# Shift and scale columns paired in one block of a modulation weight, depth steps released two at a time, latent rows ahead of context rows

## The chip, the cores and the metric

The kernel runs on one core of a Trainium2 chip. The metric is the device time of one execution in microseconds (us), and its median over several runs. Engines: PE (TensorE, the matrix engine), DVE (VectorE), ACT (ScalarE), POOL (GpSimd) and SP (SyncE, which here only issues DMAs).

## The reference, cut to what matters

One layer of a transformer over 512 latent tokens (`SEQ`) and 256 context tokens (`CTX`) of width 2048. It begins with a modulated RMS norm, and this is the only part that the change touches:

```python
mod_lat = (silu(c) @ w_mod + b_mod).reshape(B, N_MOD, 1, D)            # latent: shift, scale, gate, shift, scale, gate
mod_ctx = (silu(c_ctx)[None] @ w_mod + b_mod).reshape(1, N_MOD, 1, D)
h  = rms_norm(x, g_norm1) * (1 + mod_lat[:, 1]) + mod_lat[:, 0]
hc = rms_norm(ctx, g_norm1) * (1 + mod_ctx[:, 1]) + mod_ctx[:, 0]
p_lat, p_ctx = h @ w_in, hc @ w_in     # columns: 512 of the latent-attention query, 320 of its key/value, then neighbourhood attention
# ... two attentions, output projection, gated residual, then an expert-choice mixture of 16 experts
```

`w_mod` is a 2048 x 12288 matrix of float32. Its first 2048 columns give the shift, the next 2048 the scale. A feature (one of the 2048 depth indices of `h`) can be modulated only when both its shift and its scale are known.

## The kernel before, in words

**Stages.** The start (to 28 us of the trace) loads the tokens transposed (`xT`, 16 depth steps of 128 partitions by 768 tokens) and sums their squares. The stage of the change follows, to 138.5 us: the shift and scale columns of the modulation, the modulated tokens, and the query projection of the latent attention. Then come the key/value and neighbourhood projections (to about 520 us), the attentions, the output projection, and from about 1141 us the experts, which end the kernel.

**The modulation.** SP loads `w_mod` in blocks of 512 columns, each in four pieces of 512 depth rows (1024 KB each, L560) into a ring of six (`MOD_RING`). A semaphore `ma_used`, counted up by PE for each piece that it has used, frees a place. `mod_quarter(pos, kq)` (L683 to L691) multiplies one piece: four matmuls of 32 x 512 outputs in four column groups of the array, which the trace counts as 8 records. After four quarters DVE copies the bank to SBUF (`take_mod`, L1549), PE turns it into columns (`mod_columns`, L702: four small matmuls with 2 moving columns, in the trace 8 records, into `MJ`), and DVE adds the bias (`mod_columns` of DVE, L1554) into `modcol`. The blocks come in the order `MOD_ORDER = [0, 4, 1, 5, 2, 6, 3, 7]`: blocks 0 to 3 are shift, 4 to 7 scale. So two positions, one shift block and one scale block, are needed before any feature is ready, and they release four depth steps at once.

**The modulated tokens.** After every second position `apply_mod(kq)` runs on DVE for the four depth steps of a group. For a depth step k it scales the 512 latent columns and the 256 context columns (L1589, semaphore `h_part`); ACT adds the shift and rounds to the fp32r format (`h_hi`, L1181, `hi_set`); DVE then makes the remainder `h_lo` (L1595, `lo_set`). The order on DVE is four scalings (two depth steps, both halves), two remainders, two scalings, and so on.

**The query projection.** `qa_step(k)` (L712 to L727) is one depth step for the four latent tiles: for each tile three matmuls of 128 x 512 (`three_passes`, L709 to L711: high x high, high x low, low x high), 12 in all, into the banks of tiles 0 to 3. It reads latent rows alone, but waits for `lo_set` of both halves of step k, and for `w_low`, the remainder of its weight block, which DVE makes (`low`, L1573) from the block that ACT has rounded (`high`, L1171). A weight block holds four depth steps.

**What sets the order.** Each engine runs its program in the written order; semaphores hold it. PE's list for this stage is written by hand around L747 to L766: positions 0 and 1 first, then for each further pair of positions the four steps of the previous group between the quarters, and the last four steps at the end. After it, a loop over `SLOTS` runs the other projections, with w_mod's later blocks done by DVE (L1642, L1647) at slots given by a table.

## Time and profile before

| | us |
|---|---|
| median of 3 runs (lowest, highest) | 2102.36 (2102.05, 2112.09) |
| the profiled execution's own time | 2099.53 |
| its span, first to last instruction | 2097.7 |
| PE busy in the span | 1952.0 (93%) |
| DVE busy | 836.2 (40%) |
| ACT busy | 427.3 (20%) |
| POOL busy | 171.5 (8%) |

PE's granted clock is 0.986 of full speed over the span. DMA moved 597.55 MB at a mean of 285 GB/s, and 427 to 428 GB/s in nearly every fortieth of the span from 1200 us on. A busy share is no limit by itself: the stage of the change is 5% of the span, and what a change there is worth is read from PE's own gaps in it and from what follows.

### The profile page before, as it was taken

The page shows a single profiled execution, that of the slowest core. Times are in us where ns is not written, and L with a number is a line of the kernel's source. Part 1 is how long each engine was busy: PE and PEld are TensorE (multiplying, and loading weights), DVE is VectorE, ACT ScalarE, POOL GpSimd, SP SyncE. Part 2 cuts the span into 40 slices and gives each one's busy share as a digit, 9 for nine tenths or more (in the row PEclk, how much of TensorE's full clock was granted, in tenths as well). Part 3 has the DMA queues.
Part 4 walks back from the last instruction along what each step waited for, and adds up shares of the span by engine and source line. Part 5 has one row for each costly group of instructions (what it writes and reads, how often), then busy time and mean ns, then how long its engine had stood idle before and what let it go on. Part 6 is the DMA issues. An engine that isn't in the chain of part 4 may idle for free.

```text
span 2097.7 us, 25991 instructions
## 1 busy us (share of the span) xinstructions
PE 1952.0 (93%) x10218; PEld 1241.5 (59%) x10218; DVE 836.2 (40%) x1721; ACT 427.3 (20%) x1141; POOL 171.5 (8%) x401
## 2 busy tenths in 40 slices
PE   4899999999999999989996999999989999998987
PEld 1578788878877777768885453534434353534432
DVE  5457887773255555534444022121303121121303
ACT  4232223222145555532222000000000000000000
POOL 0003112011133222200000000000000000000000
PEclk9999999999999999999997999999999999999998
DMA  9937888783122111222227899999999999999998
GB/s 403 404 145 274 318 301 291 273 283 141 36 103 83 44 44 44 71 105 86 100 100 297 356 391 406 428 428 427 427 428 428 427 428 428 427 428 428 427 428 311
DMA packets 75208, 597.55 MB, mean 285 GB/s; under 512 B 7360, under 2 KB 25024, under 8 KB 32336
## 3 DMA queue, kind: packets, MB, share of 16 engines
q1 hardware_dynamic: 62496, 586.92, 69.4%
q10 hardware_dynamic: 12592, 8.98, 1.3%
q8 instruction: 82, 1.34, 0.3%
q14 instruction: 38, 0.31, 0.0%
HBM read 583.27 MB, written 12.60 MB: 284 GB/s over the span
## 4 chain that ended last, share of the span: by engine, by line
PE 44%; DMA 10%; DVE 2%; issue 1%; ACT 0%; POOL 0%; POOLq 0%; ACTq 0%; DVEq 0%
PE SM L1089 8%; DMA arena<-in_w_gate_up 8%; PE TM L1089 8%; PE TM L1117 5%; PE SM L1117 5%; PE TR L1047 3%; PE MJ L1047 3%; DMA arena<-in_w_down 1%; PE SN L1076 1%; PE SM L951 1%; PE SM L953 1%; PE SM L952 1%; PE TM L951 1%; PE TM L953 1%; PE TM L952 1%; DMA wor<-in_w_out 1%
## 5 line engine op out<-in xcount | busy, mean ns | idle before, releaser
L1089 PE MATMUL SM<-arena 128*64 128x512 f32 x1024 | 244.8, 598 | 35.7 <-DMA arena<-in_w_gate_up 35.2
L1089 PE MATMUL TM<-arena 128*64 128x512 f32 x1024 | 242.5, 592 | 0.0
L1647 DVE SCALAR_TENSOR_TENSOR arena<-arena,csil 128x512 f32<-128x512 f32 x240 | 180.4, 752 | 43.8 <-DMA arena<-in_w_mod 35.5
L1089 PEld LDWEIGHTS SM<-arena 128*64 128x64 f32 x1024 | 70.5, 136 | 177.0 <-issue 175.9
L1089 PEld LDWEIGHTS TM<-arena 128*64 128x64 f32 x1024 | 76.7, 137 | 143.1 <-issue 138.4
L1117 PE MATMUL TM<-arena 128*64 128x512 f32 x512 | 116.9, 598 | 1.4 <-DMA arena<-in_w_down 1.2
L1117 PE MATMUL SM<-arena 128*64 128x512 f32 x512 | 114.6, 601 | 0.9 <-DVE arena L1959 0.9
L1383 ACT CAST y_hi<-arena 128x512 fp32r<-128x512 f32 x32 | 19.8, 619 | 385.7 <-DVE arena L1920 385.1
L1171 ACT ACTIVATE wh<-wr 128x2048 fp32r<-128x2048 f32 (+1 forms) x32 | 58.7, 1835 | 192.4 <-PE TN L711 148.8
L709 PE MATMUL SM<-wh,h_hi 128*128 128x512 f32 (+1 forms) x224 | 89.5, 400 | 7.9 <-DVE h_lo L1595 7.9
L1389 ACT CAST memberT<-MJ 128x512 fp32r<-128x512 f32 x8 | 4.7, 586 | 428.3 <-PE MJ L1062 428.3
L709 PE MATMUL TM<-wh,h_hi 128*128 128x512 f32 (+1 forms) x224 | 87.5, 391 | 0.0
L1941 DVE TENSOR_TENSOR arena<-arena,SN 128x512 f32<-128x512 f32 x56 | 38.5, 687 | 122.1 <-PE SN L1077 122.1
L710 PE MATMUL SM<-wl,h_hi 128*128 128x512 f32 (+1 forms) x224 | 86.0, 384 | 0.0
L711 PE MATMUL SM<-wh,h_lo 128*128 128x512 f32 (+1 forms) x224 | 85.9, 383 | 0.0
L711 PE MATMUL TM<-wh,h_lo 128*128 128x512 f32 (+1 forms) x224 | 85.3, 381 | 0.0
L710 PE MATMUL TM<-wl,h_hi 128*128 128x512 f32 (+1 forms) x224 | 85.2, 380 | 0.0
L1409 POOL TENSOR_TENSOR st<-st,halves 128x1 f32<-128x1 f32 (+2 forms) x116 | 81.8, 705 | 41.7 <-DVE st L1562 32.1
L1573 DVE TENSOR_TENSOR wl<-wr,wh 128x2048 fp32r<-128x2048 f32 (+1 forms) x32 | 70.0, 2188 | 33.6 <-ACT wh L1171 33.5
L1895 DVE TENSOR_TENSOR arena<-cst,rope_t 128x512 f32<-128x512 f32 x8 | 5.5, 692 | 178.9 <-PE MJ L1062 178.8
L1117 PEld LDWEIGHTS SM<-arena 128*64 128x64 f32 x512 | 35.6, 138 | 68.7 <-issue 65.2
L1117 PEld LDWEIGHTS TM<-arena 128*64 128x64 f32 x512 | 33.9, 136 | 66.7 <-issue 63.2
(318 smaller groups left out, 3509.6 us busy)
## 6 DMA issues: line engine op xcount, KB each, us to landing
arena<-in_w_gate_up SPq DMA_DIRECT2D x128, 2048.0 KB, 17.4
arena<-in_w_down SPq DMA_DIRECT2D x64, 2048.0 KB, 25.5
arena<-in_w_mod SPq DMA_DIRECT2D x96, 1024.0 KB, 5.0
wr<-in_w_na SPq DMA_DIRECT2D x24, 1024.0 KB, 6.9
wor<-in_w_out SPq DMA_DIRECT2D x8, 2048.0 KB, 7.8
xT<-in_tokens_t SPq DMA_DIRECT2D x4, 1536.0 KB, 12.8
arena<-in_w_qkv SPq DMA_DIRECT2D x8, 640.0 KB, 5.1
wr<-in_w_qa SPq DMA_DIRECT2D x4, 1024.0 KB, 12.1
```

Of the source, the lines that this page charges most:

```text
L709: pe.matmul(dst, h_hi[:, k, rows], w_hi[w % 2][:, cols], start=first, stop=False)
L710: pe.matmul(dst, h_hi[:, k, rows], w_lo[w % 3][:, cols], start=False, stop=False)
L711: return pe.matmul(dst, h_lo[:, k, rows], w_hi[w % 2][:, cols], start=False, stop=last)
L951: pe.matmul(bank(n), mix_hi[:, k, cols], wo_hi[p % 2][:, i, :], start=(i == 0), stop=False)
L952: pe.matmul(bank(n), mix_hi[:, k, cols], wo_lo[p % 2][:, i, :], start=False, stop=False)
L1047: mm = pe.matmul(dst[:, i * P:(i + 1) * P], x1[:, tile, k * P:(k + 1) * P], member[:, tile, :], start=(tile == 0), stop=(tile == LT - 1))
L1089: mm = pe.matmul(GU[b][64 * e:64 * e + CAP, :], xsT[:, k, 64 * e:64 * e + CAP], w[:, 2 * (b // 2) + e, (b % 2) * NB:(b % 2 + 1) * NB], sta ...
L1117: mm = pe.matmul(GU[2 * (i // 4) + b][64 * e:64 * e + CAP, :], actT[:, f, 64 * e:64 * e + CAP], w[:, 2 * j + e, b * NB:(b + 1) * NB], star ...
L1171: sc.activation(w_hi[w % 2][:, 0:n], w_raw[w % 3][:, 0:n], ACT.Copy).then_inc(w_high, 1)
L1409: po.tensor_tensor(out_ap, ms, halves[:, 0:n], ALU.pow).then_inc(done, 1)
L1573: ve.tensor_tensor(w_lo[w % 3][:, 0:n], w_raw[w % 3][:, 0:n], w_hi[w % 2][:, 0:n].bitcast(F32), ALU.subtract).then_inc(w_low, 1)
L1647: ve.scalar_tensor_tensor(acc, row, c, acc, ALU.mult, ALU.add).then_inc(mod_step, 1)
```

## The change

The columns of `w_mod` for shift and scale are laid out anew on the host: each block of 512 columns now holds 256 shift columns and the 256 scale columns of the same features. So every position gives both for two depth steps (`MOD_K = 2`), and `MOD_ORDER` is gone. DVE computes `mul1` for two steps at every position and applies them at once. Within a position it goes latent scaling of both steps, latent remainder, context scaling, latent remainder, context scaling, then (at even positions) the weight remainder `low`, then both context remainders. `qa_step(k)` waits for the latent remainders alone; the context ones are waited for once, at the first context tile of the key/value projection (slot 4). PE runs two `qa_step` between the quarters of every position from 1 on; at the last position one of them comes after `mod_columns`. SP issues the weight block for pos//2 ahead of the pieces of positions 2, 4 and 6 instead of behind them.

```diff
--- before.py
+++ after.py
@@ -56,7 +56,7 @@
 assert ROWS == NA_KH and P % ROWS == 0
 
 MOD_RING = 6
-MOD_ORDER = [0, 4, 1, 5, 2, 6, 3, 7]
+MOD_K = KD // (2 * MODB)
 
 HALO = NA_KW // 2 * ROWS
 WIN = P + 2 * HALO
@@ -552,14 +552,16 @@
 
             for kq in range(4):
                 sp.dma_start(xT[:, 4 * kq:4 * kq + 4, :], t["tokens_t"][kq].rearrange("p (k n) -> p k n", n=TOK)).then_inc(tok_in[kq], 16)
-            for pos, b in enumerate(MOD_ORDER):
+            for pos in range(2 * MODB):
+                if pos and pos % 2 == 0:
+                    load_w(pos // 2)
                 for kq in range(4):
                     n = 4 * pos + kq
                     if n >= MOD_RING:
                         sp.wait_ge(ma_used, n - MOD_RING + 1)
-                    sp.dma_start(mod_a[n % MOD_RING], mod_piece(b, kq)).then_inc(ma_in[n % MOD_RING], 16)
-                if pos % 2 == 0:
-                    load_w(pos // 2)
+                    sp.dma_start(mod_a[n % MOD_RING], mod_piece(pos, kq)).then_inc(ma_in[n % MOD_RING], 16)
+                if pos == 0:
+                    load_w(0)
             load_w(4)
             sp.wait_ge(ma_used, 8 * MODB)
 
@@ -717,7 +719,7 @@
                     pe.wait_ge(rb_copied, 1)
                 if j == 0:
                     pe.wait_ge(w_low, kq + 1)
-                pe.wait_ge(lo_set, 2 * k + 2)
+                pe.wait_ge(lo_set, 4 * (k // MOD_K) + k % MOD_K + 1)
                 for tile in range(LT):
                     mm = three_passes(bank(tile), k, tile, kq, j, Q_RANK, k == 0, k == KD - 1)
                     if k == KD - 1:
@@ -744,26 +746,21 @@
                 dst = RSTD_BANK[:, tile * P:(tile + 1) * P] if tile < LT else TR[:, (tile - LT) * P:(tile - LT + 1) * P]
                 pe.matmul(dst, ones[:], diag[tile % 2], start=True, stop=True).then_inc(rb_full, 1)
             mod_columns(0)
-            for kq in range(4):
-                mod_quarter(1, kq)
-            mod_columns(1)
-            for pos in range(2, 2 * MODB, 2):
-                k = 2 * pos - 4
+            for pos in range(1, 2 * MODB):
+                k = MOD_K * (pos - 1)
                 mod_quarter(pos, 0)
                 mod_quarter(pos, 1)
                 qa_step(k)
                 mod_quarter(pos, 2)
-                qa_step(k + 1)
                 mod_quarter(pos, 3)
-                qa_step(k + 2)
-                mod_quarter(pos + 1, 0)
-                qa_step(k + 3)
-                mod_columns(pos)
-                for kq in range(1, 4):
-                    mod_quarter(pos + 1, kq)
-                mod_columns(pos + 1)
-            for k in range(KD - 4, KD):
-                qa_step(k)
+                if pos + 1 < 2 * MODB:
+                    qa_step(k + 1)
+                    mod_columns(pos)
+                else:
+                    mod_columns(pos)
+                    qa_step(k + 1)
+            qa_step(KD - 2)
+            qa_step(KD - 1)
 
 
             def turn(n):
@@ -834,6 +831,8 @@
                     n = first_acc(w) + tile
                     if tile == 0:
                         pe.wait_ge(w_low, w + 1)
+                    if s == LT:
+                        pe.wait_ge(lo_set, 2 * KD)
                     if w % 4 == 0 and n >= 6:
                         before = n - 6
                         if before < V_ACC:
@@ -1175,12 +1174,14 @@
             sc.copy(rstd_b[:, SEQ:TOK], TR[:, 0:CTX]).then_inc(rb_copied, 1)
             high(0)
 
-            for k in range(KD):
+            for pos in range(2 * MODB):
                 for c, (lo, hi) in enumerate(((0, SEQ), (SEQ, TOK))):
-                    sc.wait_ge(h_part, 2 * k + c + 1)
-                    sc.activation(h_hi[:, k, lo:hi], xT[:, k, lo:hi], ACT.Identity, bias=modcol[:, k, c:c + 1]).then_inc(hi_set, 1)
-                if k % 4 == 3:
-                    high(k // 4 + 1)
+                    for i in range(MOD_K):
+                        k = MOD_K * pos + i
+                        sc.wait_ge(h_part, 4 * pos + 2 * c + i + 1)
+                        sc.activation(h_hi[:, k, lo:hi], xT[:, k, lo:hi], ACT.Identity, bias=modcol[:, k, c:c + 1]).then_inc(hi_set, 1)
+                if pos % 2:
+                    high(pos // 2 + 1)
 
 
             def squares(n):
@@ -1549,10 +1550,12 @@
                 ve.tensor_copy(moda_sum, MODBANK[pos % 2]).then_inc(ma_sum, 1)
 
             def mod_columns(pos):
-                b = MOD_ORDER[pos]
+                two = slice(MOD_K * pos, MOD_K * pos + MOD_K)
                 ve.wait_ge(ma_col, pos + 1)
-                ve.tensor_tensor(modcol[:, 4 * b:4 * b + 4, :], MJ[:, 0:8].rearrange("p (a b) -> p a b", b=2),
-                                 bcol[:, 4 * b:4 * b + 4].unsqueeze(2).broadcast_to([P, 4, 2]), ALU.add).then_inc(ma_free, 1)
+                ve.tensor_tensor(modcol.rearrange("p (s k) c -> p s k c", s=2)[:, :, two, :],
+                                 MJ[:, 0:8].rearrange("p (s k c) -> p s k c", s=2, k=MOD_K),
+                                 bcol.rearrange("p (s k) -> p s k", s=2)[:, :, two].unsqueeze(3).broadcast_to([P, 2, MOD_K, 2]),
+                                 ALU.add).then_inc(ma_free, 1)
 
             ve.wait_ge(ss_step, 1)
             ve.tensor_copy(rowsum[0:1, 0:SEQ], RSTD_BANK[0:1, :])
@@ -1574,34 +1577,38 @@
 
             HALVES = ((0, SEQ), (SEQ, TOK))
 
-            def apply_mod(kq):
-                four = slice(4 * kq, 4 * kq + 4)
-                scale = slice(KD + 4 * kq, KD + 4 * kq + 4)
-                ve.wait_ge(ma_free, 2 * kq + 2)
-                ve.scalar_tensor_tensor(mul1[:, four, :], modcol[:, scale, :], 1.0, g1[:, four].unsqueeze(2).broadcast_to([P, 4, 2]),
-                                        ALU.add, ALU.mult).then_inc(mul_set, 1)
-                ve.wait_ge(mul_set, kq + 1)
-                if kq == 0:
-                    ve.wait_ge(rb_copied, 1)
-                for k in range(4 * kq, 4 * kq + 5):
-                    if k < 4 * kq + 4:
-                        for c, (lo, hi) in enumerate(HALVES):
-                            ve.scalar_tensor_tensor(xT[:, k, lo:hi], xT[:, k, lo:hi], mul1[:, k, c:c + 1], rstd_b[:, lo:hi],
-                                                    ALU.mult, ALU.mult).then_inc(h_part, 1)
-                    j = k - 1
-                    if j >= 4 * kq:
-                        for c, (lo, hi) in enumerate(HALVES):
-                            ve.wait_ge(hi_set, 2 * j + c + 1)
-                            ve.scalar_tensor_tensor(h_lo[:, j, lo:hi], xT[:, j, lo:hi], modcol[:, j, c:c + 1], h_hi[:, j, lo:hi].bitcast(F32),
-                                                    ALU.add, ALU.subtract).then_inc(lo_set, 1)
+            def scale_part(pos, c, i):
+                k, (lo, hi) = MOD_K * pos + i, HALVES[c]
+                ve.scalar_tensor_tensor(xT[:, k, lo:hi], xT[:, k, lo:hi], mul1[:, k, c:c + 1], rstd_b[:, lo:hi],
+                                        ALU.mult, ALU.mult).then_inc(h_part, 1)
+
+            def low_part(pos, c, i):
+                k, (lo, hi) = MOD_K * pos + i, HALVES[c]
+                ve.wait_ge(hi_set, 4 * pos + 2 * c + i + 1)
+                ve.scalar_tensor_tensor(h_lo[:, k, lo:hi], xT[:, k, lo:hi], modcol[:, k, c:c + 1], h_hi[:, k, lo:hi].bitcast(F32),
+                                        ALU.add, ALU.subtract).then_inc(lo_set, 1)
 
             for pos in range(2 * MODB):
+                two = slice(MOD_K * pos, MOD_K * pos + MOD_K)
+                scale = slice(KD + MOD_K * pos, KD + MOD_K * pos + MOD_K)
                 take_mod(pos)
                 mod_columns(pos)
-                if pos % 2:
-                    apply_mod(pos // 2)
-                else:
+                ve.wait_ge(ma_free, pos + 1)
+                ve.scalar_tensor_tensor(mul1[:, two, :], modcol[:, scale, :], 1.0, g1[:, two].unsqueeze(2).broadcast_to([P, MOD_K, 2]),
+                                        ALU.add, ALU.mult).then_inc(mul_set, 1)
+                ve.wait_ge(mul_set, pos + 1)
+                if pos == 0:
+                    ve.wait_ge(rb_copied, 1)
+                scale_part(pos, 0, 0)
+                scale_part(pos, 0, 1)
+                low_part(pos, 0, 0)
+                scale_part(pos, 1, 0)
+                low_part(pos, 0, 1)
+                scale_part(pos, 1, 1)
+                if pos % 2 == 0:
                     low(pos // 2)
+                low_part(pos, 1, 0)
+                low_part(pos, 1, 1)
             low(4)
             ve.tensor_scalar(gq_b[:], gq_b[:], MLA_SCALE, None, ALU.mult).then_inc(gains_set, 1)
             ve.tensor_scalar(gqn[:], gqn[:], NA_SCALE, None, ALU.mult).then_inc(gains_set, 1)
@@ -2047,6 +2054,8 @@
         "bcol": columns(g["b_mod"][:2 * D]), "bcol2": columns(g["b_mod"][3 * D:5 * D]),
     }
     w_in = g["w_in"]
+    paired = np.arange(2 * D).reshape(2, 2 * MODB, NB // 2).swapaxes(0, 1).reshape(-1)
+    w_mod = g["w_mod"][:, np.concatenate([paired, np.arange(2 * D, 6 * D)])]
     qb = to_rows(g["w_qb"].reshape(Q_RANK, HEADS, QK).swapaxes(0, 1), HEADS)
     kvb = to_rows(g["w_kvb"].reshape(KV_RANK, HEADS, NOPE + VD).swapaxes(0, 1), HEADS)
     gate, up = (g[k].reshape(PAIRS, 2, KD, P, F_EXP) for k in ("w_gate", "w_up"))
@@ -2056,7 +2065,7 @@
         "tokens_t": to_rows(tokens.T, 4),
         "c_col": np.concatenate([columns(np.asarray(inputs["c"])[0]), columns(inputs["c_ctx"])], axis=1),
         "consts": np.concatenate([consts[n].astype(np.float32) for n, _ in CONST_SIZES], axis=1),
-        "w_mod": to_rows(g["w_mod"].reshape(D, 6 * MODB, NB).swapaxes(0, 1), 6 * MODB, 4),
+        "w_mod": to_rows(w_mod.reshape(D, 6 * MODB, NB).swapaxes(0, 1), 6 * MODB, 4),
         "b_mod": np.asarray(inputs["b_mod"]),
         "w_qa": to_rows(w_in[:, :Q_RANK], 4),
         "w_kv": to_rows(w_in[:, Q_RANK:IN_MLA], 4),
```

On PE, at the first positions before: two groups of `mod_columns` (`L702`), with position 1's 16 quarter matmuls between them, then two quarters of position 2 (`TM` is its bank, `csil` the activations) and the first query step, whose first three matmuls are shown.

```order
L702 MATMUL MJ<-cst,arena 128x2 x4
L690 MATMUL TN<-arena,csil 32x512 x16
L702 MATMUL MJ<-cst,arena 128x2 x4
L690 MATMUL TM<-arena,csil 32x512 x8
L709 MATMUL SM<-wh_62,h_hi 128x512
L710 MATMUL SM<-wl_59,h_hi 128x512
L711 MATMUL SM<-wh_62,h_lo 128x512
```

The same place now, with the lines of the changed kernel (`L704` is `L702` of before, `L692` is `L690`, `L711` to `L713` are `L709` to `L711`):

```order
L704 MATMUL MJ<-cst,arena 128x2 x4
L692 MATMUL TN<-arena,csil 32x512 x8
L711 MATMUL SM<-wh_62,h_hi 128x512
L712 MATMUL SM<-wl_59,h_hi 128x512
L713 MATMUL SM<-wh_62,h_lo 128x512
```

The first query step has moved ahead past the other two quarters of position 1, its columns, and two quarters of position 2: it now stands after two quarters of position 1.

On DVE, the first group before, from the second columns to the first remainders (`xT` the tokens, `mul` the scale, `wl_59` a weight remainder, `h_lo` the tokens' remainder):

```order
L1573 TENSOR_TENSOR wl_59<-wr_56,wh_62 128x2048
L1549 COPY arena<-TN 128x512
L1554 TENSOR_TENSOR modcol<-MJ,cst 128x8
L1581 SCALAR_TENSOR_TENSOR mul<-modcol,cst 128x8
L1589 SCALAR_TENSOR_TENSOR xT<-xT,mul,rstd_b 128x512
L1589 SCALAR_TENSOR_TENSOR xT<-xT,mul,rstd_b 128x256
L1589 SCALAR_TENSOR_TENSOR xT<-xT,mul,rstd_b 128x512
L1589 SCALAR_TENSOR_TENSOR xT<-xT,mul,rstd_b 128x256
L1595 SCALAR_TENSOR_TENSOR h_lo<-xT,modcol,h_hi 128x512
```

The same place now, a whole even position (512 wide is latent, 256 context):

```order
L1555 TENSOR_TENSOR modcol<-MJ,cst 128x2x4
L1597 SCALAR_TENSOR_TENSOR mul<-modcol,cst 128x4
L1582 SCALAR_TENSOR_TENSOR xT<-xT,mul,rstd_b 128x512 x2
L1588 SCALAR_TENSOR_TENSOR h_lo<-xT,modcol,h_hi 128x512
L1582 SCALAR_TENSOR_TENSOR xT<-xT,mul,rstd_b 128x256
L1588 SCALAR_TENSOR_TENSOR h_lo<-xT,modcol,h_hi 128x512
L1582 SCALAR_TENSOR_TENSOR xT<-xT,mul,rstd_b 128x256
L1576 TENSOR_TENSOR wl_59<-wr_56,wh_62 128x2048
L1588 SCALAR_TENSOR_TENSOR h_lo<-xT,modcol,h_hi 128x256 x2
```

Two operations less stand ahead of the first latent remainder, and the weight remainder `wl_59` has moved from the front of position 0 to behind six token operations of it.

## Rows read from the trace of the kernel before

**Rows 1.** Windows of stages: us, busy by engine, PE clock, DMA share, GB/s.

```profile
71.00:97.00 26.00, 23.19 (x135) 13.60 (x138) 12.73 (x23) 6.23 (x9) 0.00 (x0) 0.93 0.97 397
97.00:121.00 24.00, 21.10 (x128) 12.12 (x120) 12.60 (x23) 6.23 (x9) 0.00 (x0) 1.00 0.67 260
121.00:138.50 17.50, 13.73 (x48) 11.15 (x49) 10.51 (x22) 7.31 (x14) 0.79 (x3) 0.80 0.36 150
138.50:440.00 301.50, 299.00 (x1485) 250.28 (x1484) 231.55 (x295) 86.38 (x257) 59.98 (x80) 1.00 0.79 280
...
60.00:72.00 12.00, 11.18 (x77) 6.58 (x79) 3.70 (x6) 0.00 (x0) 0.00 (x0) 1.00 1.01 421
...
112.00:116.00 4.00, 4.00 (x27) 2.97 (x19) 0.00 (x0) 0.00 (x0) 0.00 (x0) 1.00 0.06 19
```

**Rows 2.** Waits of PE between 26 and 140 us: total, times, longest.

```profile
PE SM L709 <- DVE h_lo L1595: 7.9, 3, 3.9
PE MJ L702 <- DVE arena L1549: 3.3, 4, 0.8
PE TM L690 <- DMA arena<-in_w_mod: 1.5, 1, 1.5
```

**Rows 3.** Waits of PE between 140 and 440 us, the longest.

```profile
PE TR L781 <- ACT arena L1235: 2.2, 4, 0.6
```

**Rows 4.** Timeline of PE, columns of position 0, quarters of position 1: start, duration.

```profile
38.28 1.05 PE L702 MATMUL MJ<-cst,arena 128*128 128x2 f32 x8
39.27 3.92 PE L690 MATMUL TN<-arena,csil 128*32 128x512 f32 x32
```

**Rows 5.** Timeline of PE around columns of position 5 and step 8.

```profile
95.82 1.05 PE L702 MATMUL MJ<-cst,arena 128*128 128x2 f32 x8 [0.81 <-DVE arena L1549]
96.80 1.92 PE L690 MATMUL TM<-arena,csil 128*32 128x512 f32 x16
100.73 0.47 PE L709 MATMUL SM<-wh,h_hi 128*128 128x512 f32 x1 [2.00 <-DVE h_lo L1595]
...
103.64 1.06 PE L690 MATMUL TM<-arena,csil 128*32 128x512 f32 x8
```

**Rows 6.** Timeline of PE: a step, a quarter, the next step.

```profile
80.60 0.50 PE L709 MATMUL SM<-wh,h_hi 128*128 128x512 f32 x1
...
83.54 1.06 PE L690 MATMUL TM<-arena,csil 128*32 128x512 f32 x8
84.54 0.50 PE L709 MATMUL SM<-wh,h_hi 128*128 128x512 f32 x1
```

**Rows 7.** Timeline of PE: last columns, starts of steps 12 and 13, key/value projection.

```profile
119.87 1.05 PE L702 MATMUL MJ<-cst,arena 128*128 128x2 f32 x8 [0.81 <-DVE arena L1549]
124.77 0.77 PE L709 MATMUL SM<-wh,h_hi 128*128 128x512 f32 x1 [3.85 <-DVE h_lo L1595]
...
130.03 0.63 PE L709 MATMUL SM<-wh,h_hi 128*128 128x512 f32 x1
...
138.53 0.30 PE L709 MATMUL TM<-wh,h_hi 128*128 128x320 f32 x1
```

**Rows 8.** Timeline of DVE: first weight remainder, and step 8's scalings and remainders.

```profile
40.91 2.29 DVE L1573 TENSOR_TENSOR wl<-wr,wh 128x2048 fp32r<-128x2048 f32 x1 [1.37 <-ACT wh L1171]
...
97.31 2.21 DVE L1589 SCALAR_TENSOR_TENSOR xT<-xT,mul,rstd_b 128x512 f32<-128x512 f32 x4
99.44 1.14 DVE L1595 SCALAR_TENSOR_TENSOR h_lo<-xT,modcol,h_hi 128x512 fp32r<-128x512 f32 x2
```

**Rows 9.** One line's instructions on DVE: ns min/median/max, first and last start.

```profile
L1595 DVE SCALAR_TENSOR_TENSOR h_lo<-xT,modcol,h_hi x32: 477/616/755, 47.6 to 129.4; 128x512 fp32r<-128x512 f32 x16, 128x256 fp32r<-128x256 f32 x16
```

**Rows 10.** Timeline of ACT: first weight block, and step 8's and 9's sums.

```profile
38.95 1.92 ACT L1171 ACTIVATE wh<-wr 128x2048 fp32r<-128x2048 f32 x1
...
98.10 2.18 ACT L1181 ACTIVATE h_hi<-xT,modcol 128x512 fp32r<-128x512 f32 x4 [17.41 <-DVE xT L1589]
```

**Rows 11.** Timeline of SP's queue: key/value weight blocks.

```profile
120.33 31.01 SPq L551 DMA_DIRECT2D wr<-in_w_kv  x3
```

## The prediction

> **What bounds the kernel now.** I read the windows by stage first, then PE's waits, then the timelines of PE, DVE and ACT in the stage of the change. From 71 to 121 us PE is busy nearly throughout while DMA falls from a share of 0.97 to 0.67, and from 112 to 116 us DMA moves almost nothing though PE still has the last quarters to do [rows 1]. So the end of this stage is set by PE and by what PE waits for, not by the weights' transfer. From 138.5 to 440 us PE is busy 299.0 of 301.5 us, with DMA at 0.79 [rows 1] and a longest group of waits of 2.2 us in all [rows 3]: whatever time the stage of the change gives to PE reaches the stages behind it, which run in PE's order. The reader should therefore ask one question: when does PE begin the key/value projection, at 138.53 us before [rows 7]?
>
> PE's waits in the stage are 7.9 us for the token remainder `h_lo` (three waits: 2.0, 2.0 and 3.85), 3.3 us for the copy of a modulation bank (four of 0.81) and 1.5 us for one piece of `w_mod` [rows 2, 5, 7], 12.7 us in all. Its clock is a second cost: the mean granted clock is 0.93 from 71 to 97 us and 0.80 from 121 to 138.5 us, against 1.00 between [rows 1]. At the tail PE idles 3.85 us, and step 12 then takes 130.03 - 124.77 = 5.26 us [rows 7], at the level of 1.2 GHz; step 8, at 2.4 GHz, takes 103.64 - 100.73 = 2.91 us [rows 5].
>
> **What the change costs and moves.** The sum of the work stays. PE has the same 32 quarters, 8 columns groups and 16 steps. DVE has the same 64 token operations and four more small `mul1` (it runs 8 instead of 4, of half the width, beside PE's quarters); ACT has the same. So the sum is PE's order walked through with the durations before.
>
> The building blocks, on PE: columns to the next quarter 96.80 - 95.82 = 0.98 us; two quarters behind columns 1.92 us [rows 5]; a step behind a quarter 83.54 - 80.60 = 2.94 us, and a quarter behind a step 84.54 - 83.54 = 1.00 us, so a pair behind a step about 1.93 us [rows 6]; a step behind a step (138.53 - 130.03) / 3 = 2.83 us [rows 7]. On DVE: the first scaling starts 97.31 - 95.82 = 1.49 us after PE's columns start [rows 5, 8]. Two token operations, one latent and one context, are issued in (99.44 - 97.31) / 2 = 1.065 us [rows 8]; they last 0.755 and 0.477 us [rows 9], so they overlap by 0.085 each, and the latent one takes 0.67 us of DVE, the context one 0.39.
>
> *One position (2 to 6).* Counted from the start of the columns before it: scalings from 1.49 us, both latent ones issued by 2.83. ACT starts its first sum 98.10 - 97.31 = 0.79 us after the first scaling, and of 2.18 us for two latent and two context sums [rows 8, 10] a latent one has some 0.67 us, so it ends at 2.95; the remainder can start at about 3.05, ends at 3.80, and PE starts 0.15 later, as before (99.44 + 1.14 to 100.73 [rows 5, 8]): 3.95. PE's own work is done at 0.98 + 1.92 = 2.90, so it waits 1.05 us. Before, the wait was 2.00 us per pair of positions, so halving the chain saves nothing over two positions; the copy's 0.81 us, however, was open once per pair and is now under a step of 2.9 us. A position is then 3.95 + 2.91 (step) + 1.93 (quarters) + 2.94 (step) = 11.73 us.
>
> *The first position.* Here the change adds a wait. The weight remainder of block 0 ran on DVE at 40.91 us [rows 8], before anything else needed DVE; now it is queued behind six token operations. DVE scales from 38.28 + 1.49 = 39.77 us [rows 4], ACT is on the weight block until 38.95 + 1.92 = 40.87 [rows 10] and then makes the first sum by 41.54, and from 41.6 DVE issues two remainders and two context scalings, 2 x 0.67 + 2 x 0.39 = 2.1 us, then the weight remainder of 2.29 us [rows 8]: 46.0, and step 0 at 46.2. PE has done its two quarters at 39.27 + 1.93 = 41.2 [rows 4] and waits 5.0 us. Behind step 0 in PE's order are quarters 6 and 7 and with them two places of the ring.
> After a longer gap than the tail's 3.85 us I take step 0 at the tail's 5.26 us [rows 7]; at full clock it would be 2.91. So: 46.2 + 5.26 + 1.93 + 2.94 = 56.3 us for the start of position 1's columns.
>
> *To the end.* Five positions: 56.3 + 5 x 11.73 = 114.9, columns of position 6. The last position: 3.95 + 2.91 + 1.93 = 8.79, and 0.81 for the copy, which no step covers here: columns at 124.5. Step 13 lies in the wait for the last remainders (0.98 + 2.94 = 3.92 against 3.95), which before stood open for 3.85 us, and steps 14 and 15 follow: 124.5 + 3.95 + 2 x 2.83 = 134.1 us. Against 138.5 that is 4.4 us gained. By kind: waits 5.0 + 6 x 1.05 + 0.81 = 12.1 us against 12.7, so almost nothing; the rest is clock, where two of the stretches at 1.2 GHz fall away (the one between 71 and 97 us and the tail's) and one comes at step 0. Bounds: step 0 at full clock gives 6.7 us; each further step at 1.2 GHz costs 5.26 - 2.91 = 2.35 us.
>
> **What hides the other edits.** *DMA:* a load of 1024 KB at 421 GB/s [rows 1] takes 2.5 us; nine per pair of positions are 22.5 us against 2 x 11.73 = 23.5 on PE. PE stays the slower. While it waits for step 0 the ring holds pieces up to the eleventh, and the queue runs on. Even if transfers set the pace, the last piece would land near 112 us as before [rows 1], ten before it is needed. Moving three weight blocks ahead of four pieces delays these by 2.5 us, inside that lead. *DVE at the end:* from 126.0 the eight token operations take 4 x 0.67 + 4 x 0.39 + 0.2 = 4.4 us, then the remainder of the first key/value block, about 1.5 us: 132, two before PE needs it at 134.1; the wait for context rows stands four tiles later and is free. *SP:* the loads of the next key/value blocks, issued at 120.33 us [rows 11], depend on the last quarter and move to about 125; two pieces and the block need 2 x 2.5 + 1.6 us, so it lands by 134, while PE wants its remainder a whole block of six tiles after 134. If these covers failed, each costs its own lateness, under 3 us.
>
> The profiled execution took 2099.5 us and lies 2.9 under the median; its sum is 2099.5 - 4.4 = 2095.1, and at the median 2102.4 - 4.4 = 2098.0 us.
>
> **Rivals.** *Full cover:* if DVE's chain is met by PE's quarters at positions 2 to 7, 6 x 1.05 = 6.3 us more go, 10.7 in all: 2091.7. For it speaks only that 1.05 us is a small difference of four durations; against it, that the same chain left 2.0 us before [rows 5]. *The clock keeps falling:* a wait and a columns group now stand ahead of every second step, not of every fourth. If PE drops to 1.2 GHz at each of the six starts, 6 x 2.35 = 14.1 us come on: 138.5 + 9.7, or 2112.1, slower. From the second fall the gain is gone. For it: between 71 and 97 us the clock fell with a wait of the same kind as the 2.00 us at 100.73, where it did not (0.93 against 1.00) [rows 1, 5]. Against it: the waits are half as long, and none of 0.81 us precedes them. The Trainium skill names this case ("TensorE: Matmul & The Clock Gate", section "A second HAM failure mode: psum-queue depth-cycling"): frequent small idles between groups of matmuls make the clock swing between its two levels. By that rule the six starts would be slow; this trace bears it out for some gaps of 2 us and more, not for all. *No change:* the stage ends earlier but a later one, paced by DVE's products of w_mod, keeps its time: 2102.4. Against it stand PE's 299.0 busy us [rows 1, 3].
>
> **Chances.** Forecast (2 to 8 us gained) 0.62; full cover 0.13; clock 0.13, mostly with two to four falls, that is 0 to 5 us slower; no change 0.12. A change of 0.5%, 10.5 us, is about what a measurement of this kernel can tell from none. The forecast and the no-change case lie inside it, full cover straddles it, and only five or more falls reach the other side. So faster 0.13, same 0.82, slower 0.05. The range reaches to 2089 (full cover, and step 0 at full clock) and to 2105 (three falls).
>
> **What would show it.** In the changed profile: a wait of about 5 us before the first query step, ended by the weight remainder; six waits near 1 us; no wait for the copy except at the last position; none behind the last columns; the key/value projection starting near 134 us; nothing new between 140 and 440 us. I am wrong if the first wait is short, if the granted clock is under 0.9 in the positions after the first, or if that projection starts early and the end of the kernel does not follow.

## The result and the profile after

The changed kernel takes 2115.59 us in the median of 13 runs (2113.69 to 2120.25), the kernel before 2104.65 us in 13 runs (2099.83 to 2112.09): a ratio of 1.0053, with a 95% interval of 1.0043 to 1.0062. It is 10.9 us slower where 4.4 us of gain were forecast.

The waits of PE from 26 to 160 us, grouped by what ended them (total, times, longest), answer to [rows 2]:

```profile
PE SM L711 <- DVE wl L1576: 18.6, 4, 4.8
PE SM L711 <- DVE h_lo L1588: 2.8, 3, 0.9
PE MJ L704 <- DVE arena L1550: 0.8, 1, 0.8
```

The 12.7 us of before have become 22.2, and the largest group is new: PE waits four times, 4.6 to 4.8 us each, for `wl`, the remainder of a weight block. The waits for the tokens' remainder that were forecast six times occur three times, and only one copy of a bank is still waited for. The windows of the stage (us, PE, PEld, DVE, ACT, POOL busy, PE clock, DMA share, GB/s), to be laid beside [rows 1]:

```profile
45.00:71.00 26.00, 23.66 (x128) 14.11 (x128) 9.92 (x20) 5.38 (x7) 0.00 (x0) 0.87 0.99 397
71.00:97.00 26.00, 21.03 (x116) 13.37 (x120) 11.24 (x21) 5.43 (x8) 0.00 (x0) 0.93 0.83 334
97.00:121.00 24.00, 18.49 (x109) 10.35 (x102) 12.21 (x21) 6.61 (x9) 0.00 (x0) 0.93 0.81 318
121.00:138.50 17.50, 12.91 (x64) 7.82 (x64) 7.63 (x12) 2.40 (x4) 0.00 (x0) 0.80 0.10 39
```

PE is busy 21.03 and 18.49 us in the two middle windows against 23.19 and 21.10 before, and the clock is 0.93 in the second of them instead of 1.00. The transfers move 334 GB/s in the first of them instead of 397, and still 318 in the second, where those of before had fallen to 260 because they were nearly done. PE waits for none of them any more, so it is PE that holds them up and not they PE. Here is PE's timeline around the start of step 4, and the start of the key/value projection:

```profile
67.65 0.95 PE L704 MATMUL MJ<-cst,arena 128*128 128x2 f32 x8
68.53 1.92 PE L692 MATMUL TN<-arena,csil 128*32 128x512 f32 x16
75.04 0.50 PE L711 MATMUL SM<-wh,h_hi 128*128 128x512 f32 x1 [4.59 <-DVE wl L1576]
...
79.57 1.92 PE L692 MATMUL TN<-arena,csil 128*32 128x512 f32 x16
...
149.02 0.30 PE L711 MATMUL TM<-wh,h_hi 128*128 128x320 f32 x1
```

And DVE in the same stretch:

```profile
68.64 0.17 DVE L1555 TENSOR_TENSOR modcol<-MJ,cst 128x8 f32<-128x8 f32 x1 [3.05 <-PE MJ L704]
68.84 0.16 DVE L1597 SCALAR_TENSOR_TENSOR mul<-modcol,cst 128x4 f32<-128x4 f32 x1
69.04 1.42 DVE L1582 SCALAR_TENSOR_TENSOR xT<-xT,mul,rstd_b 128x512 f32<-128x512 f32 x2
70.58 0.75 DVE L1588 SCALAR_TENSOR_TENSOR h_lo<-xT,modcol,h_hi 128x512 fp32r<-128x512 f32 x1
71.25 0.48 DVE L1582 SCALAR_TENSOR_TENSOR xT<-xT,mul,rstd_b 128x256 f32<-128x256 f32 x1
71.64 0.74 DVE L1588 SCALAR_TENSOR_TENSOR h_lo<-xT,modcol,h_hi 128x512 fp32r<-128x512 f32 x1
72.31 0.48 DVE L1582 SCALAR_TENSOR_TENSOR xT<-xT,mul,rstd_b 128x256 f32<-128x256 f32 x1
72.70 2.28 DVE L1576 TENSOR_TENSOR wl<-wr,wh 128x2048 fp32r<-128x2048 f32 x1
74.91 0.87 DVE L1588 SCALAR_TENSOR_TENSOR h_lo<-xT,modcol,h_hi 128x256 fp32r<-128x256 f32 x2
```

The tokens' remainder that step 4 needs is done at 70.58 + 0.75 = 71.33 us. PE starts the step at 75.04, a moment after the weight remainder of block 1 ends, which DVE takes up only at 72.70. DVE had stood idle for 3.05 us ahead of 68.64. The step needs both, and in DVE's order both stand behind the same columns. (The weight remainder needs no columns itself; only its place in the order makes it wait for them.) In the kernel before the weight remainder came in the position before, under PE's quarters.

From there on nothing new happens: between 145 and 440 us the longest group of waits answers to [rows 3] to the tenth:

```profile
PE TR L778 <- ACT arena L1236: 2.2, 4, 0.6
```

The ledger to the key/value projection, 149.02 - 138.53 = 10.5 us: waits 22.2 - 12.7 = 9.5. The first steps of the four weight blocks (0, 4, 8, 12) took 4.00, 4.50, 2.91 and 5.26 us before, 5.39, 4.53, 4.49 and 5.42 now: 3.2 more, by the clock. The other 2.2 us come back in quarters that ran slow before (the first two of position 2) and in columns with no idle time ahead. The stage's 10.5 us are nearly the whole loss by the medians, 10.9. The profiled spans differ by more, 2112.1 - 2097.7 = 14.4; 2.7 of that arise between 590 and 611 us, where the clock of this execution was 0.83 and that of before 1.00. Attention's first scores are 10.5 later, its last 13.2 (line 876 before, 875 now: 575.3 to 904.6 and 585.8 to 917.8 us). Nothing ties that to the change: the scores stretch over 332.0 us here and over 330.8 to 332.5 us in the profiles of all eight experiments below, the faster ones too, so the 329.3 us of the one profiled execution of before are the odd ones out. From the start of the key/value projection to the first scores it is 436.7 to 436.9 us in all ten profiles.

### The profile page after: what moved, and what is told of

Read it like the earlier page. It is cut to its first block, busy times and chain, and to the rows that moved or that the text cites. A ratio compares the mean times of both kernels' runs of the same rounds, so it can differ in the third digit from the quotient of the medians.

```text
span 2112.1 us, 25996 instructions
## 1 busy us (share of the span) xinstructions
PE 1957.1 (93%) x10218; PEld 1245.9 (59%) x10218; DVE 838.3 (40%) x1725; ACT 428.5 (20%) x1141; POOL 171.6 (8%) x401
## 4 chain that ended last, share of the span: by engine, by line
PE 44%; DMA 9%; DVE 2%; issue 0%; ACT 0%; DVEq 0%; ACTq 0%
PE SM L1088 8%; DMA arena<-in_w_gate_up 8%; PE TM L1088 8%; PE TM L1116 5%; PE SM L1116 5%; PE TR L1046 3%; PE MJ L1046 3%; DMA arena<-in_w_down 1%; PE SN L1075 1%; PE TM L950 1%; PE TM L952 1%; PE TM L951 1%; PE SM L950 1%; PE SM L952 1%; PE SM L951 1%; PE TN L1075 1%
## 5 line engine op out<-in xcount | busy, mean ns | idle before, releaser
L711 PE MATMUL SM<-wh,h_hi 128*128 128x512 f32 (+1 forms) x224 | 90.3, 403 | 21.4 <-DVE wl L1576 18.6
L711 PE MATMUL TM<-wh,h_hi 128*128 128x512 f32 (+1 forms) x224 | 87.8, 392 | 0.0
L713 PE MATMUL SM<-wh,h_lo 128*128 128x512 f32 (+1 forms) x224 | 86.8, 387 | 0.0
L713 PE MATMUL TM<-wh,h_lo 128*128 128x512 f32 (+1 forms) x224 | 85.4, 381 | 0.0
## 6 DMA issues: line engine op xcount, KB each, us to landing
arena<-in_w_gate_up SPq DMA_DIRECT2D x128, 2048.0 KB, 17.4
xT<-in_tokens_t SPq DMA_DIRECT2D x4, 1536.0 KB, 12.7
```

Source lines behind the costliest of these rows:

```text
L711: pe.matmul(dst, h_hi[:, k, rows], w_hi[w % 2][:, cols], start=first, stop=False)
L713: return pe.matmul(dst, h_lo[:, k, rows], w_hi[w % 2][:, cols], start=False, stop=last)
```

## Experiments

Theory A: the loss is the place of the weight remainder on DVE, and the slow steps behind the waits that it makes. Rival B: the clock falls because the gaps on PE come twice as often. Rival C: the new order of SP's loads. Each run's ratio is to the kernel before on the same chip. The starts of the key/value projection given below carry up to 1.2 us that arise ahead of the stage: the columns of position 0 start at 37.04 to 38.28 us in the ten profiles.

### The weight remainders moved out of the chain

```diff
-                if pos % 2 == 0:
-                    low(pos // 2)
+                if pos == 0:
+                    low(0)
                 low_part(pos, 1, 0)
                 low_part(pos, 1, 1)
-            low(4)
+                if pos % 2:
+                    low(pos // 2 + 1)
```

> Only the place of the weight remainders for blocks 1 to 4 is changed: from inside the token operations of the even positions to behind those of the odd positions. Theory A (PE's 4.6 us waits before steps 4, 8 and 12 are these remainders, queued on DVE behind six token operations): the three waits fall to the 0.93 us of the other positions, 11.0 us, and the stretches at 1.2 GHz behind them go with them, up to 5.6 us more; key/value projection starts at 132 to 135 us instead of 149.0, kernel 2099 to 2102 us. Rival B (what costs is the clock, which swings because gaps come twice as often, whatever ends them): the waits go but the clock falls stay, 2104 to 2106 us. Rival C (the order of transfers on SP costs): no change, 2115 us.

Measured: 2098.43 us, ratio 0.9966 (0.9954 to 0.9979); key/value projection at 131.84 us. PE's waits in the stage:

```profile
PE SM L711 <- DVE h_lo L1588: 5.9, 6, 1.0
PE SM L711 <- DVE wl L1576: 4.8, 1, 4.8
PE MJ L704 <- DVE arena L1550: 0.8, 1, 0.8
```

and DVE at the end of position 1, where it used to idle:

```profile
63.15 2.29 DVE L1576 TENSOR_TENSOR wl<-wr,wh 128x2048 fp32r<-128x2048 f32 x1 [1.32 <-ACT wh L1170]
65.36 0.68 DVE L1550 COPY arena<-TM 128x512 f32<-128x512 f32 x1
68.09 0.17 DVE L1555 TENSOR_TENSOR modcol<-MJ,cst 128x8 f32<-128x8 f32 x1 [2.04 <-PE MJ L704]
```

The same instruction, 2.29 us long, now ends before the columns come, and costs PE nothing. There are six waits of 0.9 to 1.0 us, and steps 1 to 15 all take 2.7 to 3.0 us: no fall of the clock behind any of them. That is A; B asked for falls that stay, C for no change. It is even a little faster than A's range for this run (2099 to 2102 us, projection from 132 us on). With the remainders of blocks 1 to 4 moved, the change does what was forecast for it, and more: the projection starts 6.7 us earlier than before where 4.4 were forecast, and by the ratio the gain is 0.34%, 7 us. That the forecast's 2098.0 us and the measured 2098.4 nearly agree is chance: on this chip the kernel before took 2105.4 us, not 2102.4.

### The suspected cause put into the kernel before

```diff
-                else:
-                    low(pos // 2)
+                elif pos == 0:
+                    low(0)
 ...
                     j = k - 1
+                    if j == 4 * kq + 1 and kq:
+                        low(kq)
```

> The kernel before with the suspected cause put into it: the weight remainders of blocks 1 to 3 stand inside the token operations of their group (behind six scalings and two remainders) instead of ahead of the second bank copy. Nothing else is changed. Theory A: steps 4, 8, 12 themselves wait as before, or step 4 starts when its weight remainder ends: 1.49 + 2.13 + 1.06 + 1.06 + 2.2 + 0.15 = 8.1 us after the columns start instead of 4.9, so 3.2 us more three times, 9.6 us, and up to 2.3 us of clock at step 8: 2114 to 2117 us. Rivals B and C (pairing, more frequent gaps, order of transfers): these are all absent here, so the time stays at 2103 to 2106 us.

Measured: 2118.95 us, ratio 1.0061 (1.0048 to 1.0073); projection at 149.92 us, 11.4 later than before. DVE's timeline behind the columns of position 3:

```profile
71.49 2.21 DVE L1589 SCALAR_TENSOR_TENSOR xT<-xT,mul,rstd_b 128x512 f32<-128x512 f32 x4
73.62 1.14 DVE L1597 SCALAR_TENSOR_TENSOR h_lo<-xT,modcol,h_hi 128x512 fp32r<-128x512 f32 x2
74.67 1.14 DVE L1589 SCALAR_TENSOR_TENSOR xT<-xT,mul,rstd_b 128x512 f32<-128x512 f32 x2
75.73 2.28 DVE L1573 TENSOR_TENSOR wl<-wr,wh 128x2048 fp32r<-128x2048 f32 x1
```

PE waits 17.4 us for `wl` in three waits, against 7.9 for `h_lo` before: 9.5 more, where 9.6 were worked out. Step 8 fell to the slow level too (5.42 us for 2.91), as the upper end of A's range allowed, and step 4 stayed in it longer (5.05 for 4.50). The stage's 11.4 us lie inside what was expected, 9.6 to 11.9; the kernel is 2 us over the expected range, and where those 2 us arise is open. With no pairing, no more gaps than before and SP's old order, this one move makes a loss as large as the change's own. That the two are equal is chance: in the changed kernel the same place costs 149.0 - 131.8 = 17.2 us, and the rest of the change gives 6.7 back.

### Each half of the change alone

Latent rows ahead of context rows in the kernel before (DVE, ACT and the wait for `lo_set`; shown is PE's wait):

```diff
-                pe.wait_ge(lo_set, 2 * k + 2)
+                pe.wait_ge(lo_set, 4 * (k // 2) + k % 2 + 1)
```

> The kernel before with only the second half of the change: latent rows ahead of context rows in DVE's and ACT's order, each step waiting for its latent remainder alone, the context ones waited for once at the first context tile. Columns are not paired, weight remainders stay where they were. Theory A: the waits before steps 4, 8 and 12 go from 2.0, 2.0, 3.85 us to 0.9, 0.9, 2.8, 3.2 us in all, and one of the falls of the clock may go (up to 1.6 us): key/value projection at 134 to 135.5 us, kernel 2100 to 2102 us. Rival B (clock alone): the fall after step 12's wait stays and nothing else is gained, 2103 to 2105 us.

Measured: 2101.33 us, ratio 0.9978 (0.9969 to 0.9987); projection at 134.0 us, 4.5 earlier. The three waits for `h_lo` are 4.9 us in all instead of 7.9, and step 4 takes 2.93 us instead of 4.50, while step 12, behind a wait of 2.88 us, still takes 4.8. Time and projection lie in A's range. Not all 4.5 us come from the edit: 1.0 arises ahead of the stage, and the waits for `w_mod` grew from 1.5 to 3.1 us.

Paired columns, weight remainders late, but both halves in one chain:

```diff
                 scale_part(pos, 0, 0)
+                scale_part(pos, 1, 0)
                 scale_part(pos, 0, 1)
+                scale_part(pos, 1, 1)
+                if pos == 0:
+                    low(0)
                 low_part(pos, 0, 0)
+                low_part(pos, 1, 0)
 ...
```

> As the run with the late weight remainders, but the token operations go in the order of the kernel before (four scalings of both halves, then remainders of both halves), ACT in that order too, and each step waits for both halves. Step 0's weight remainder stands behind the four scalings. So it is the pairing of columns without the latent rows ahead. Theory A: the chain to a step is that of before, a wait of 2.0 us at each of six positions instead of 0.93, that is 6.4 us more than with latent rows ahead, less 0.6 at step 0: 2105 to 2108 us, the time of before or a little over. Rival B: the longer gaps bring the clock down at more starts, 2110 us and more. If latent rows ahead are worth nothing: the time of the run before this one.

Measured: 2111.21 us, ratio 1.0027 (1.0018 to 1.0036); projection at 145.1 us. Here my A was too low and B's figure is met. PE's waits are 16.8 us for `h_lo` in eight waits and 0.8 for the copy, 17.6 in all, against 11.5 in the late-remainder run (5.9 + 4.8 + 0.8): 6.1 more, where 6.4 - 0.6 = 5.8 were worked out. But the projection is 13.3 us later. The rest is clock: of the six steps behind waits of about 2 us (2, 4, 6, 8, 10, 12) five took 4.4 to 4.5 us, one 2.94. The windows:

```profile
71.00:97.00 26.00, 22.10 (x116) 14.21 (x112) 11.34 (x19) 5.64 (x9) 0.00 (x0) 0.87 0.87 336
...
121.00:138.50 17.50, 14.69 (x80) 9.33 (x79) 8.00 (x18) 3.72 (x7) 0.00 (x0) 0.90 0.17 62
```

So here gaps at every position bring the clock down when they are 2 us long, and do not when they are 1 us. Pairing by itself makes the kernel slower even with its remainders in the right place; with the shorter chain it does not. What pairing adds to the shorter chain is small: both together give 0.9966, the chain alone in the kernel before 0.9978, and the two intervals overlap.

### The clock alone

```diff
                 mod_quarter(pos, 1)
+                if pos in (3, 5, 7):
+                    for _ in range(18):
+                        pe.matmul(MODBANK[0], h_hi[:, 0, 0:P], h_hi[:, 0, 0:NB], start=True, stop=True)
                 qa_step(k)
```

> The changed kernel with 18 extra matmuls of 128x512 on PE (some 4.1 us at full clock) ahead of steps 4, 8 and 12, into a bank that is free then; they fill the 4.6 us waits and are no part of the computation. Theory A: the waits themselves are not shortened (DVE sets them), but the clock does not fall, so steps 4, 8 and 12 take 2.9 us instead of 4.53, 4.49 and 5.42: 5.7 us less, key/value projection at about 143.5 us instead of 149.0, kernel 2109 to 2111 us. If the clock stays low whatever PE does, or the steps' length has another cause (DVE and PE reading the same memory): 2115 us or more.

Measured: 2106.82 us, ratio 1.0013 (1.0005 to 1.0022); projection at 142.97 us, 6.05 earlier than in the changed kernel.

```profile
70.16 4.42 PE L755 MATMUL TM<-h_hi 128*128 128x512 f32 x18
74.81 0.50 PE L711 MATMUL SM<-wh,h_hi 128*128 128x512 f32 x1 [0.24 <-DVE wl L1579]
...
77.76 1.92 PE L692 MATMUL TN<-arena,csil 128*32 128x512 f32 x16
```

DVE still sets the start (74.81 us for 75.04), but step 4 takes 77.76 - 74.81 = 2.95 us instead of 4.53, and the granted clock from 71 to 140 us is 1.00. The same data, banks and DVE work beside it: the steps' length follows what PE does in the 4.6 us ahead of them, and nothing else that changed. By the ratios the gain over the changed kernel is 0.0040 of 2104 us, 8.4, more than the stage's 6.05 (and the kernel 2 us below A's range of 2109 to 2111); what the other 2.4 are is open.

### SP's order put back

```diff
-                if pos and pos % 2 == 0:
-                    load_w(pos // 2)
 ...
-                if pos == 0:
-                    load_w(0)
+                if pos % 2 == 0:
+                    load_w(pos // 2)
```

> The changed kernel with the order of SP's loads put back to that of before (weight block behind the pieces of positions 2, 4 and 6). Theory A: nothing, 2114 to 2117 us. Rival C (that order costs): up to 2.5 us per pair of positions come back, 2106 to 2109 us.

Measured: 2114.96 us, ratio 1.0053 (1.0040 to 1.0066), the ratio of the changed kernel to the digit; projection at 148.27 us. Rival C is out.

### The first wait, and one quarter more ahead of each step

The first wait was forecast. Taking it on as well, on top of the late remainders:

```diff
                 scale_part(pos, 0, 1)
+                if pos == 0:
+                    low(0)
                 low_part(pos, 0, 0)
 ...
                 mod_quarter(pos, 1)
-                qa_step(k)
+                if pos > 1:
+                    qa_step(k)
                 mod_quarter(pos, 2)
                 mod_quarter(pos, 3)
+                if pos == 1:
+                    qa_step(k)
```

> The run with late weight remainders, and the last long wait taken on too: the weight remainder of block 0 stands behind the two latent scalings (while ACT makes the first sum), and PE does all four quarters of position 1 ahead of step 0. Theory A: DVE 39.6 + 1.4 + 2.2 + 0.7 gives step 0 at about 44.1 us instead of 45.5, PE has work to 43.0, so the wait goes from 4.8 to about 1.1 us and the fall of the clock behind it (2.4 us) goes; step 1 ends at 44.1 + 2.9 + 2.9 = 49.9 instead of 55.6. Key/value projection at 126 to 129 us, kernel 2093 to 2096 us. If the clock falls all the same: 2096 to 2097 us. If DMA becomes the bound instead: PE waits for w_mod appear and the time stays near 2098 us.

Measured: 2091.49 us, ratio 0.9940 (0.9928 to 0.9952); projection at 124.88 us, step 0 at 43.16 us and 2.81 us long. The projection is 1 to 4 us earlier and the kernel 1.5 us faster than I expected. 0.9 us of it arises ahead of the stage (columns of position 0 at 37.24 us for 38.11). DVE's first token remainder is done at 43.02 us and PE's fourth quarter at 43.16, so the wait for DVE before step 0 is gone, and so is the fall of the clock behind it; a wait of 1.1 us for `w_mod` now stands ahead of that fourth quarter.

Then three quarters ahead of the first step at positions 2 to 6, and four at the last:

```diff
-                mod_quarter(pos, 0)
-                mod_quarter(pos, 1)
-                if pos > 1:
-                    qa_step(k)
+                for kq in range(3):
+                    mod_quarter(pos, kq)
 ...
```

> The run before this one, with three quarters of a position ahead of the first step of positions 2 to 6 and four at the last. Theory A: PE's own work then reaches 3.8 us behind the columns start, against 3.9 for DVE's chain, so the six waits of 0.93 us fall to 0.1 to 0.2 (4.6 us) and the copy's 0.8 us at the last position is covered: 5.4 us less than the run before. But nine loads of 2.5 us per two positions are 22.5 us and PE then needs about 21.7, so the transfers take over as the bound: the last piece lands no sooner than 110 to 112 us, then a quarter, a step, the columns and three steps, 12.6 us: key/value projection at 122 to 125 us, kernel 2088 to 2092 us, with waits of PE for w_mod.

Measured: 2088.60 us, ratio 0.9924 (0.9913 to 0.9936); projection at 123.71 us. The waits of PE from 36 to 130 us:

```profile
PE TM L692 <- DMA arena<-in_w_mod: 3.5, 3, 1.3
PE TN L692 <- DMA arena<-in_w_mod: 1.3, 2, 0.9
PE SM L711 <- DVE h_lo L1592: 1.0, 3, 0.7
```

The waits for `h_lo` fell from 5.4 us to 1.0 and the one for the copy went, 5.2 us; 3.7 of them came back as waits for `w_mod` (4.8 against 1.1), so the projection starts only 1.2 us earlier. The transfers are the bound now: DMA's share is 1.01 from 39 to 97 us at 420 to 422 GB/s. It is the fastest kernel of this study, 0.76% under the kernel before. The intervals of the two ratios overlap, but they share the same runs of the kernel before; the five times of this run (2085.4 to 2089.6 us) all lie under the five of the run before it (2090.3 to 2093.0) on the same chip, so the last step gains some 3 us.

## Why the prediction was wrong

*What bounds the kernel: right.* The stage is paced by PE and its waits, and what it loses reaches the end: 10.5 us at the projection, 10.9 in the medians, and across the ten kernels the order of the projection's starts (123.7 to 149.9 us) is that of the times (2088.6 to 2119.0).

*The first position: right.* Its columns come at 56.2 us, 56.3 forecast. 5.0 us of wait forecast, 4.84 measured, ended by the weight remainder; step 0 at 5.26 us, measured 5.39.

*One position (2 to 6): this step failed.* It counted the chain from the columns to the step as two scalings, ACT's sum and one remainder, 3.95 us, for all five positions and the last. I had placed the weight remainder in that chain at position 0 and then dropped it, though the order printed ahead of the prediction shows it inside "a whole even position". Steps 4, 8 and 12 stand at positions 3, 5 and 7, right behind the columns of even positions, and so wait for the remainder that DVE makes there. Three waits of 4.59 us instead of the forecast 1.05 are 10.6 us; the clock behind them adds (4.53 + 4.49 + 5.42) - 3 x 2.91 = 5.7. My 134.1 and these two give 150.4, against 149.0 measured. Against the late-remainder run the account closes: 3 x (4.59 - 0.93) + 5.7 = 16.7 of 17.2 us, and 0.4 more arise ahead of the stage. The positions without a remainder came out a little shorter than forecast: in the late-remainder run 11.44 to 11.50 us instead of 11.73, with waits of 0.93 to 1.03 instead of 1.05. That, 0.7 us at the first position (0.5 of it ahead of the stage) and 0.3 us at the end are the 2.3 us by which that run beats my 134.1.

The extra 3.66 us per wait are more than the remainder's own 2.28: three token operations stand between the one that the step needs and the weight remainder.

*"By kind: waits almost nothing, the rest is clock": right in kind once the remainder is out.* In the late-remainder run, which is the forecast carried out, the waits are 11.5 us against 12.7 before. Of its 6.7 us at the projection, the waits give 1.2, the steps 0, 4, 8 and 12 give 16.7 - 14.1 = 2.6, and the two quarters ahead of step 0, 3.5 us before, give 1.6. I had counted two slow stretches in the kernel before; it has a third, which my windows did not show, from 46 to 52 us:

```profile
45.00:52.00 7.00, 5.54 (x22) 2.01 (x22) 6.84 (x15) 3.73 (x7) 0.00 (x0) 0.52 1.02 419
```

So the slow stretch at step 0, which I booked as new, was already there.

*The clock rival came out at 2112.1 us, near the 2115.6 measured, by another mechanism.* It wanted a fall at every start behind waits of 1 us. Behind such waits ahead of a step the clock did not fall once: not at the three of the changed kernel, nor at the six of the late-remainder run, nor at the six of the run with quarters first (0.65 to 1.03 us). It fell behind all three of 4.6 us. The Trainium skill's rule that frequent small idles make the clock swing ("TensorE: Matmul & The Clock Gate", section "A second HAM failure mode: psum-queue depth-cycling") is borne out by the pairing-alone run, where it fell at five of six waits of about 2 us, and not by waits of 1 us.

*The covers: right.* DMA, SP's order and the end on DVE cost nothing, by the run with SP's order put back and by the wait list after 145 us.

*What a measurement can tell: too coarse.* I took 0.5% for about the least that it tells from none; the intervals came out at 0.1% to either side, and the change's 0.53% is well clear of them.

## What to carry to other kernels

When a chain on an in-order engine is repriced, walk every consumer in every position through all the semaphores that it waits for, not through the one that the change is about: a helper's operation queued inside the chain costs its own time, and that of whatever stands ahead of it, wherever its consumer is next. Where a change gives back a few us, look for the work that it moves from an idle stretch into a busy one. Here 2.3 us of DVE work placed three times behind the columns instead of ahead of them turned a gain of 0.34% into a loss of 0.53%.

In this stage a wait of PE cost twice where it was long enough to bring the clock down: six waits of 2 us instead of 1 cost 5.8 us of waiting and 7.8 of clock. Where a wait cannot be shortened, what PE does in it still counts: the filler run got 6 us back with matmuls that compute nothing.

## What the runs showed of the hardware

In this stage, where a wait ahead of a step follows four small column matmuls and two quarters (at the tail of the old order the columns alone), the wait's length went with the granted clock behind it:

- waits of 0.65 to 1.03 us left it at 2.4 GHz in all 23 cases (six kernels: the changed one, late remainders, latent alone, filler, SP's order back, quarters first);
- waits of 1.9 to 2.0 us brought it to 1.2 GHz in five of six cases in the pairing-alone kernel and in one of two in the kernel before;
- waits of 2.9 us and more brought it there in all 16 cases (eight kernels).

A slow step behind such waits takes 4.4 to 5.4 us instead of 2.9. The price of a 2 us wait was thus about 3.6 us in five of the six cases of the pairing-alone kernel, which I had not expected.

The wait's length alone is not the whole of it. In the kernel before the clock fell between 45 and 46 us, behind a wait of 0.81 us and the columns, while a quarter ran, and ahead of the wait of 1.46 us that follows. Up to there PE had run columns and quarters alone since 38.3 us, and no step. No run here tells what made that difference.
